# Loading the input by channel instead of transposing it, and shorter arithmetic in the norms, in a hybrid decoder layer

## The chip, the cores and the metric

The kernel runs on one core of one Trainium2 chip. The metric is the device time of one execution in microseconds (us), the median over several executions. Lower is better.

## What is computed

One decoder layer on 256 tokens of 2048 channels, all in float32, batch 1. Three sub-layers follow one another, and each ends in a layer norm over a scaled residual:

```python
h = x
h = _layer_norm(DEEPNORM_ALPHA * h + 0.5 * _swiglu(h, ffn1_w_gate, ffn1_w_up, ffn1_w_down), ln_ffn1_g, ln_ffn1_b)
mix = _mixer(h, ...)      # sparse attention and dilated attention, gated and projected
h = _layer_norm(DEEPNORM_ALPHA * h + mix, ln_mix_g, ln_mix_b)
h = _layer_norm(DEEPNORM_ALPHA * h + 0.5 * _swiglu(h, ffn2_w_gate, ffn2_w_up, ffn2_w_down), ln_ffn2_g, ln_ffn2_b)
```

`_swiglu(x)` is `(silu(x @ w_gate) * (x @ w_up)) @ w_down` with a hidden width of 5632. `_layer_norm` subtracts the mean, multiplies by `rsqrt(var + 1e-5)`, then by a vector g, and adds a vector b. The mixer adds two small position tables (32 x 128) to windows of keys and values before it compresses them.

## The kernel before

**The products.** Every large product multiplies activations that lie with channels on the partitions (`act_hi`, `act_lo`, `hT_hi`, `hT_lo`) with weights that come from HBM. float32 precision is kept by splitting both sides: hi is the value rounded to float32r, lo is the rest. A product is hi x hi, lo x hi and hi x lo, so each pair of a 128x128 block of activations and a 128x512 block of weights takes three matmuls.

**Slots.** Weights come in slots of 2 x 128 rows and 512 columns (512 KB). SyncE (SP) issues one load for each slot into a ring `raw` of 4 (`load_slot`, L469). ScalarE (ACT) rounds a slot into `w_hi` (`round_slot`, L491), VectorE (DVE) writes the rest into `w_lo` (`split_slot`, L505), and TensorE (PE) does 12 matmuls on it (`multiply_slot`, L511, or `first_chunk_slot`, L1625, for the first eight slots). Three waits tie the engines together. The load of slot n waits until the split of slot n-4 is done (`lo_done`, L471). The rounding of slot n waits until PE has used slot n-4 (`slots_used`, L501). The split waits for the rounding, PE for both.

**Order of the first stage.** A feed-forward stage (`ffn`) takes 11 chunks of 512 hidden columns. A chunk is 8 slots of the gate's weights (half 0) and 8 slots of the up weights (half 1), so chunk 0 is slots 0 to 15. After slot 9 has been rounded, ACT takes the tanh of the gate's sums (L841), which waits for PE to have used slot 7, and DVE multiplies by it (L1070); only then come the roundings and splits of slots 10 and 11. Chunk 0 of the first stage is written out by hand ("peel"), the other ten are a loop. Then four chunks of 22 slots each go through the down weights and are added to the residual `resid` (`add_chunk`).

**The input.** x is loaded by token into `resid`, in five pieces of columns (`load_x`, L705) that SP issues between the first slots. PE transposes it, two blocks of channels at a time (`x_task`, L1584: four 128x128 transposes each, eight tasks in all), into PSUM banks. ACT rounds a pair into `act_hi` (L598), DVE writes the rest into `act_lo` (L608). The transposes need the identity `ident`, SP's second load (L717). While no input is there PE multiplies zeros (`keep_warm`, L1610), 6 times before the first transposes and 5 times after them.

**The vectors.** g and b of the first two norms and both position tables are loaded as rows (`load_vectors`, L734, six loads after the load of slot 4). `setup_task` (L1704), right after slot 7 on PE, transposes them into a bank, and DVE copies them into `vecT` (L1059). The same vectors are also loaded broadcast over all partitions into `ln_nat` (`load_ln`, L756), for the residual; SP issues the first pair of these, 1 MB each as written, right after the load of slot 15.

**Norms.** DVE sums the last columns, takes statistics and adds eps to the variance (`sum_last`, `variance`), ACT takes the square root s (`deviation`), and DVE corrects 1/s by one Newton step: a reciprocal and three small operations that wait for one another (`inverse_deviation`, L1159). The last norm (`last_norm`, L1187) multiplies (x - mean) by g over 512 and then over 1536 columns (`scaled`), while ACT does the correction in four small steps (`factor`, L899). Then four `finish` operations of 512 columns multiply by the factor and add b; after each of them SP or ACT, in turns, stores that piece of 256 KB.

**Bank order.** `plan` numbers all uses of the four PSUM banks ahead of time; engines wait for those numbers.

Of the kernel before, what the change touches and what calls it, by code (L numbers as in the profile page):

```python
# [49 lines left out]
X_PARTS = ((0, 256), (256, 512), (512, 1024), (1024, 1536), (1536, D))  # L50
# [76 lines left out]
class Plan:  # L127


    def __init__(self):  # L130
        self.k, self.uses, self.t, self.at, self.by_pos = 0, [0] * BANKS, {}, {}, {}
        self.turn = list(range(BANKS))
# [9 lines left out]
def plan():  # L142
# [10 lines left out]
    def ffn(f):  # L153
        for j in range(GU_SLOTS):
            task(("x", f, j), j % BANKS)
        if f == 0:
            task(("setup",), 2)
# [100 lines left out]
def build(nc, x, w1_gate, w1_up, w1_down, ln1_g, ln1_b, w_in, ck_pos, ck_w1, ck_w2, cv_pos, cv_w1, cv_w2,  # L258
          w_a, w_b, w_o, ln2_g, ln2_b, w2_gate, w2_up, w2_down, ln3_g, ln3_b, rope_c, masks_c, small_c, out):

    (w1_gate, w1_up, w1_down, ln1_g, ln1_b, w_in, ck_pos, ck_w1, ck_w2, cv_pos, cv_w1, cv_w2, w_a, w_b, w_o,
     ln2_g, ln2_b, w2_gate, w2_up, w2_down, ln3_g, ln3_b) = (
        a[0] for a in (w1_gate, w1_up, w1_down, ln1_g, ln1_b, w_in, ck_pos, ck_w1, ck_w2, cv_pos, cv_w1, cv_w2,
# [4 lines left out]
    with ctx:  # L268
# [9 lines left out]
        pos_rows = sb("pos_rows", [CMP_BLOCK, 2, P])  # L278
# [5 lines left out]
        at = 1152 + 4 * (160 + 128 + 256 + 128 + 48 + 16 + 8)  # L284
# [69 lines left out]

        def chunk_buf(order):
            b = CHUNK_BUF[order]
            return chunks_lo[:, b] if b < 8 else chunks_hi[:, b - 8]
# [32 lines left out]
        x_loaded = [sem(f"x_loaded{q}") for q in range(len(X_PARTS))]  # L390
# [12 lines left out]
        three_halves = sem("three_halves")  # L403
# [300 lines left out]
        def _(sp):  # L704
            def load_x(q):  # L705
                cs = slice(*X_PARTS[q])
                sp.dma_start(resid[:, :, cs], x[0].rearrange("(t p) d -> p t d", p=P)[:, :, cs]) \
                    .then_inc(x_loaded[q], 16)
# [25 lines left out]
            def load_vectors():  # L734
                for v, a in enumerate((ln1_g, ln1_b, ln2_g, ln2_b)):
                    sp.dma_start(vec_rows[16 * v:16 * v + 16, :], a.rearrange("(t p) -> t p", p=P)) \
                        .then_inc(consts_loaded, 16)
                sp.dma_start(pos_rows[:, 0, :], ck_pos).then_inc(consts_loaded, 16)
                sp.dma_start(pos_rows[:, 1, :], cv_pos).then_inc(consts_loaded, 16)
# [75 lines left out]
            for tile in range(TILES):  # L815
                for n in range(0, len(OUT_PIECES), 2):
# [5 lines left out]
        def _(act):  # L822
            def gu_chunk(f, i, peel):
                per, c0 = 2 * GU_SLOTS, gu_acc[f]
                for s in range(2 * GU_SLOTS):
                    if peel and f == 0 and s <= X_FIRST:
# [5 lines left out]
                    if peel and f == 0 and X_FIRST < s < GU_SLOTS:  # L832
                        x_pairs(s)
# [26 lines left out]
            def x_pairs(j):  # L860

                round_pair(act, ("x", 0, j), pair_of(act_hi, 2 * j))
# [30 lines left out]
            def deviation(which, tile):  # L893
# [3 lines left out]
                                     bias=ln_s[:, 6, which % 2:which % 2 + 1]).then_inc(std_ready, 1)  # L897

            def factor(tile):  # L899

                at = slice(tile, tile + 1)
                var, r, t, inv = (ln_s[:, k, at] for k in (0, 1, 2, 3))
                act.wait_ge(three_halves, 1)
                act.wait_ge(recip_ready, tile + 1)
                nc.scalar.activation(t, var, ACT.Copy, scale=r).then_inc(factor_step, 1)
                act.wait_ge(factor_step, 4 * tile + 1)
                nc.scalar.activation(t, t, ACT.Copy, scale=r).then_inc(factor_step, 1)
                act.wait_ge(factor_step, 4 * tile + 2)
                nc.scalar.activation(t, t, ACT.Identity, scale=-0.5, bias=ln_s[:, 7, 1:2]).then_inc(factor_step, 1)
                act.wait_ge(factor_step, 4 * tile + 3)  # L910
                nc.scalar.activation(inv, r, ACT.Copy, scale=t).then_inc(factor_step, 1)

            def layer_norm_act(which):

                f, n0 = ("mix", 1)[which], (mix_slot, gu_slot[1])[which]
                for s in range(SPARE):
# [109 lines left out]
            for tile in range(TILES):  # L1026
                deviation(2, tile)
                factor(tile)
                for n in range(1, len(OUT_PIECES), 2):
# [4 lines left out]
        def _(dve):  # L1034
# [8 lines left out]
            def gu_chunk(f, i, peel):  # L1043
                per = 2 * GU_SLOTS
                for s in range(2 * GU_SLOTS):
                    if peel and f == 0 and s <= X_FIRST:
# [5 lines left out]
                    if peel and f == 0 and X_FIRST < s < GU_SLOTS:  # L1052
                        x_pairs(s)
                    if peel and f == 1 and SPLIT <= s < GU_SLOTS:
                        split_piece(1, s + SPLIT)
                    if f == 0 and peel and s == 11:
# [999 lines left out]
```

## Time and profile before

| | |
|---|---|
| median of 3 runs | 2217.81 us (2217.52 to 2217.85) |
| the profiled execution's own time | 2217.98 us |
| its span, from the first instruction to the last | 2216.2 us |
| PE busy | 2201.7 us (99%) |
| DVE, ACT, POOL busy | 1235.7, 959.6, 7.7 us |
| mean granted clock of TensorE | 0.998 of full speed |
| HBM read, mean rate | 418 MB, 190 GB/s over the span |

A time of the profile is counted from the start of the span. What lies outside the span is 2217.98 - 2216.2 = 1.8 us. A busy engine is one that has an instruction in work; matmuls are pipelined, so that the sum of their durations is longer than the time from one start to the next. Two facts of the listing matter below: a float32 matmul of zeros (L1613) leaves two records, and issues of loads stand under SPq and ACTq, the sequencers.

### The profile page before, as it was taken

How to read it: one execution, taken by the hardware profiler on the slowest of the kernel's cores; microseconds unless marked ns; L12 is line 12 of the kernel's file. 1: busy time of each engine (PE TensorE's matmuls, PEld its weight loads, DVE VectorE, ACT ScalarE, POOL GpSimd, SP SyncE). 2: the span in 40 equal slices, each digit the busy share in tenths (PEclk: the TensorE clock that was granted, in tenths of full speed). 3: DMA queues.
4: the chain of work that ended last, by engine and by line, in shares of the span. 5: the costliest groups of instructions: out<-in, count | busy, mean ns of one | idle time of the engine just before them, and what ended most of it. 6: DMA issues, size and time to landing. Idle time of an engine off the chain costs nothing.

```text
span 2216.2 us, 27207 instructions
## 1 busy us (share of the span) xinstructions
PE 2201.7 (99%) x10137; PEld 1823.6 (82%) x10137; DVE 1235.7 (56%) x1230; ACT 959.6 (43%) x1126; POOL 7.7 (0%) x12
## 2 busy tenths in 40 slices
PE   9999999999999999999999999999999999999998
PEld 7888888888888888888888888888888888888886
DVE  5555455544544776776654556567555545545445
ACT  4344434443333644544345444364444444443333
POOL 0000000000000010000000000000000000000000
PEclk9999999999999999999999999999999999999999
DMA  7655665565666666665557566656655566566664
GB/s 270 206 184 188 190 191 185 188 191 190 195 192 193 186 188 206 188 184 161 169 163 208 171 204 206 196 166 195 197 188 180 188 197 188 180 236 193 196 191 142
DMA packets 224860, 422.86 MB, mean 191 GB/s; under 512 B 16400, under 2 KB 25872, under 8 KB 224016
## 3 DMA queue, kind: packets, MB, share of 16 engines
q1 hardware_dynamic: 224208, 420.76, 61.7%
q8 instruction: 52, 0.85, 0.2%
q10 hardware_dynamic: 576, 1.05, 0.1%
q14 instruction: 24, 0.20, 0.0%
HBM read 418.08 MB, written 3.68 MB: 190 GB/s over the span
## 4 chain that ended last, share of the span: by engine, by line
PE 98%; DVE 1%; ACT 0%; DMA 0%; issue 0%; SPq 0%; DVEq 0%; ACTq 0%
PE acc L519 31%; PE acc L520 31%; PE acc L525 31%; PE bank L558 1%; PE bank L1903 1%; PE bank L1743 0%; PE bank L1852 0%; PE bank L1874 0%; PE acc L1640 0%; PE acc L1641 0%; PE bank L1957 0%; PE acc L1647 0%; PE bank L1954 0%; DMA raw<-in_ffn_w_gate_dram 0%; PE bank L1856 0%; DVE w_lo L509 0%
## 5 line engine op out<-in xcount | busy, mean ns | idle before, releaser
L509 DVE TENSOR_TENSOR w_lo<-raw,w_hi 128x1024 fp32r<-128x1024 f32 x768 | 928.3, 1224 | 572.3 <-ACT w_hi L502 564.5
L502 ACT ACTIVATE w_hi<-raw 128x1024 fp32r<-128x1024 f32 x766 | 802.9, 1059 | 820.9 <-PE acc L525 775.0
L519 PE MATMUL acc<-w_hi,act_hi 128*128 128x512 f32 x2192 | 865.9, 395 | 0.0
L520 PE MATMUL acc<-w_hi,act_lo 128*128 128x512 f32 x2192 | 854.3, 390 | 0.0
L525 PE MATMUL acc<-w_lo,act_hi 128*128 128x512 f32 x2192 | 588.2, 389 | 0.1
L525 PEld LDWEIGHTS acc<-w_lo,act_hi 128*128 128x128 f32 x2192 | 411.3, 188 | 87.4 <-DVE w_lo L509 1.0
L519 PEld LDWEIGHTS acc<-w_hi,act_hi 128*128 128x128 f32 x2192 | 411.7, 188 | 86.7 <-issue 3.2
L520 PEld LDWEIGHTS acc<-w_hi,act_lo 128*128 128x128 f32 x2192 | 411.9, 188 | 82.1
L519 PE MATMUL acc<-w_hi,hT_hi 128*128 128x512 f32 x688 | 267.9, 389 | 0.0
L520 PE MATMUL acc<-w_hi,hT_lo 128*128 128x512 f32 x688 | 267.7, 389 | 0.0
L525 PE MATMUL acc<-w_lo,hT_hi 128*128 128x512 f32 x688 | 185.2, 389 | 0.0
L525 PEld LDWEIGHTS acc<-w_lo,hT_hi 128*128 128x128 f32 x688 | 129.2, 188 | 26.8
L520 PEld LDWEIGHTS acc<-w_hi,hT_lo 128*128 128x128 f32 x688 | 129.2, 188 | 26.7
L519 PEld LDWEIGHTS acc<-w_hi,hT_hi 128*128 128x128 f32 x688 | 129.1, 188 | 26.7
L1089 DVE TENSOR_TENSOR hT_lo<-bank,hT_hi 128x512 f32 (+1 forms) x44 | 30.3, 688 | 97.2 <-ACT hT_hi L858 97.2
L1070 DVE SCALAR_TENSOR_TENSOR gate_t<-gate_t,acc 128x1024 f32<-128x1024 f32 x22 | 26.9, 1222 | 88.7 <-ACT gate_t L841 88.7
L858 ACT ACTIVATE hT_hi<-bank 128x512 f32 (+1 forms) x44 | 26.2, 595 | 108.0 <-PE bank L558 108.0
L1081 DVE TENSOR_TENSOR hid<-gate_t,acc 128x1024 f32<-128x1024 f32 x22 | 26.9, 1222 | 65.0 <-PE acc L525 65.0
L841 ACT ACTIVATE gate_t<-acc 128x1024 f32<-128x1024 f32 x22 | 22.6, 1029 | 92.1 <-PE acc L525 90.1
L519 PE MATMUL acc<-w_hi,oT_hi 128*128 128x512 f32 x96 | 38.0, 395 | 0.0
L520 PE MATMUL acc<-w_hi,oT_lo 128*128 128x512 f32 x96 | 37.4, 390 | 0.0
L689 ACT ACTIVATE s<-s,negmax 128x128 f32<-128x128 f32 (+1 forms) x56 | 23.8, 430 | 26.8 <-DVE negmax L1310 26.8
(243 smaller groups left out, 842.2 us busy)
## 6 DMA issues: line engine op xcount, KB each, us to landing
raw<-in_ffn_w_up_dram SPq DMA_DIRECT2D x176, 512.0 KB, 4.5
raw<-in_ffn_w_down_dram SPq DMA_DIRECT2D x176, 512.0 KB, 4.5
raw<-in_w_in_dram SPq DMA_DIRECT2D x176, 512.0 KB, 4.2
raw<-in_ffn_w_gate_dram SPq DMA_DIRECT2D x174, 512.0 KB, 4.5
raw<-in_w_o_dram SPq DMA_DIRECT2D x32, 512.0 KB, 4.8
raw<-in_w_branch_a_dram SPq DMA_DIRECT2D x16, 512.0 KB, 5.1
raw<-in_cmp_k_w_dram SPq DMA_DIRECT2D x8, 512.0 KB, 4.0
raw<-in_cmp_v_w_dram SPq DMA_DIRECT2D x8, 512.0 KB, 4.0
```

Of the source, the lines that this page charges most:

```text
L502: nc.scalar.activation(weights(n0, s if isinstance(i, int) and i == 0 else s + per)[0], raw[:, r, :], ACT.Copy).then_inc(hi_done, 1)
L509: nc.vector.tensor_tensor(lo, raw[:, r, :], hi.bitcast(F32), ALU.subtract).then_inc(lo_done, 1)
L519: nc.tensor.matmul(o, a_hi[:, kt0 + k, at], hi, start=first and k == 0, stop=False)
L520: nc.tensor.matmul(o, a_lo[:, kt0 + k, at], hi, start=False, stop=False)
L525: mm = nc.tensor.matmul(o, a_hi[:, kt0 + k, at], lo, start=False, stop=last and k == SLOT_KT - 1)
L558: mm = nc.tensor.transpose(bank[:, b, k * TOKENS + tile * P:k * TOKENS + (tile + 1) * P], src[:, tile, col + k * P:col + (k + 1) * P], ident)
L689: nc.scalar.activation(v, v, ACT.Exp, bias=negmax[:, u, e:e + 1], scale=SCALE, accum_out=sums[:, u, e:e + 1]).then_inc(probs_ready, 1)
L841: nc.scalar.activation(gate_t[:, :, :], acc_pair(0), ACT.Tanh, scale=0.5).then_inc(gate_tanh, 1)
L858: nc.scalar.activation(dst, bank[:, half, :].rearrange("p (k n) -> p k n", k=2), ACT.Copy).then_inc(hi_moved, 1)
L1070: nc.vector.scalar_tensor_tensor(gate_t[:, :, :], gate_t[:, :, :], 1.0, acc_pair(0), ALU.add, ALU.mult).then_inc(acc_emptied[0], 1)
L1081: nc.vector.tensor_tensor(hid[:, :, :], gate_t[:, :, :], acc_pair(1), ALU.mult).then_inc(acc_emptied[1], 1)
L1089: nc.vector.tensor_tensor(hT_lo[:, k0, :], bank[:, half, :].rearrange("p (k n) -> p k n", k=2), hT_hi[:, k0, :].bitcast(F32), ALU.subtract ...
```

## The change

- The host hands over x a second time, rearranged so that a partition holds a channel (`x_by_channel`), and one array `vectors` that has g, b and the position tables in the layout of `vecT`. The original x is still an input.
- SP loads x by channel into `x_raw`, which lies in the space of `hT_hi`, in eight loads of 256 KB, each ahead of the load of the slot that uses it. ACT rounds from there into `act_hi` (512 columns each) and DVE writes the rest into `act_lo`; no transposes. On ACT and DVE the pair of slot s comes ahead of slot s for all eight (before, from slot 3 on, behind it).
- PE's eight `x_task`s and the `setup_task` are gone, and with them the copy L1059. PE multiplies zeros 8 times. In the first eight slots PE does the hi x hi of both tiles before the lo x hi, with a wait for `act_lo` between.
- The identity and the vectors are loaded after the load of slot 15, ahead of the broadcast vectors. PE waits for the identity right after slot 7, where `setup_task` was.
- x by token is loaded whole (2 MB) between the gate/up loop and the down slots of the first stage; the first `add_chunk` waits for it.
- Norms: ACT takes the square root of a quarter of the variance, s/2; the factor is 1 / (s/2 + (v/4) / (s/2)). That is a reciprocal, one operation and a reciprocal on DVE; in the last norm the middle one is on ACT, in place of four there, and DVE takes the second reciprocal.
- The last norm scales and finishes in turns: scale 0 to 512, scale 512 to 1024, finish both, scale and finish 1024 to 1536, scale 1536 to 2048, finish 256 columns and 256 columns. Five stores in place of four.

```diff
-OUT_PIECES = ((0, 512), (512, 1024), (1024, 1536), (1536, D))
+OUT_PIECES = ((0, 512), (512, 1024), (1024, 1536), (1536, 1792), (1792, D))
-WARM_START = (6, 5)
-X_FIRST = 2
+WARM_START = 8
...
@@ @block.sync @@
-            def load_x(q):
-                cs = slice(*X_PARTS[q])
-                sp.dma_start(resid[:, :, cs], x[0].rearrange("(t p) d -> p t d", p=P)[:, :, cs]) \
-                    .then_inc(x_loaded[q], 16)
+            def load_x(j):
+                sp.dma_start(pair_of(x_raw, 2 * j), xT_c[:, 2 * j * TOKENS:(2 * j + 2) * TOKENS]).then_inc(x_loaded[j], 16)
...
-            load_x(0)
-            sp.dma_start(ident, small_c[:, n_small:]).then_inc(small_loaded, 16)
...
+                        if peel:
+                            load_x(s)
                         if peel and s < IN_HALVES:
                             first_weights(s)
                         else:
                             load_slot(sp, src, gu_slot[f], i, 2 * GU_SLOTS, h * GU_SLOTS + s)
-                        if peel:
-                            for q in ((1,), (2,), (), (3, 4))[s] if s < 4 else ():
-                                load_x(q)
-                            if s == 4:
-                                load_vectors()
...
+            def load_constants():
+                sp.dma_start(ident, small_c[:, n_small:]).then_inc(small_loaded, 16)
+                sp.dma_start(vecT[:, :], vec_c).then_inc(consts_loaded, 16)
 
             def ffn(f):
                 gu_chunk(f, 0)
                 if f == 0:
+                    load_constants()
                     load_ln(0)
                 with sp.Fori(1, GU_CHUNKS) as i:
                     gu_chunk(f, i)
-                if f == 1:
+                if f == 0:
+                    sp.dma_start(resid[:, :, :], x[0].rearrange("(t p) d -> p t d", p=P)).then_inc(resid_loaded, 16)
+                else:
                     sp.wait_ge(resid_ready, 2)
                     load_ln(2)
...
@@ @block.scalar @@
             def x_pairs(j):
 
-                round_pair(act, ("x", 0, j), pair_of(act_hi, 2 * j))
+                act.wait_ge(x_loaded[j], 16)
+                nc.scalar.activation(pair_of(act_hi, 2 * j), pair_of(x_raw, 2 * j), ACT.Copy).then_inc(hi_moved, 1)
...
             def factor(tile):
...
+                quarter_var, r, t, half_std = (ln_s[:, k, tile:tile + 1] for k in (0, 1, 2, 5))
                 act.wait_ge(recip_ready, tile + 1)
-                nc.scalar.activation(t, var, ACT.Copy, scale=r).then_inc(factor_step, 1)
-                act.wait_ge(factor_step, 4 * tile + 1)
-                nc.scalar.activation(t, t, ACT.Copy, scale=r).then_inc(factor_step, 1)
-                act.wait_ge(factor_step, 4 * tile + 2)
-                nc.scalar.activation(t, t, ACT.Identity, scale=-0.5, bias=ln_s[:, 7, 1:2]).then_inc(factor_step, 1)
-                act.wait_ge(factor_step, 4 * tile + 3)
-                nc.scalar.activation(inv, r, ACT.Copy, scale=t).then_inc(factor_step, 1)
+                nc.scalar.activation(t, quarter_var, ACT.Identity, scale=r, bias=half_std).then_inc(factor_step, 1)
...
@@ @block.vector @@
             def x_pairs(j):
 
-                split_pair(dve, ("x", 0, j), pair_of(act_lo, 2 * j), pair_of(act_hi, 2 * j))
+                dve.wait_ge(hi_moved, moved[("x", 0, j)] + 1)
+                nc.vector.tensor_tensor(pair_of(act_lo, 2 * j), pair_of(x_raw, 2 * j), pair_of(act_hi, 2 * j).bitcast(F32),
+                                        ALU.subtract).then_inc(x_split, 1)
...
-                link(nc.vector.reciprocal(r, ln_s[:, 5, at]))
-                link(nc.vector.scalar_tensor_tensor(t, r, var, r, ALU.mult, ALU.mult))
-                link(nc.vector.tensor_scalar(t, t, -0.5, 1.5, ALU.mult, ALU.add))
-                link(nc.vector.tensor_tensor(inv, r, t, ALU.mult))
+                link(nc.vector.reciprocal(r, half_std))
+                link(nc.vector.scalar_tensor_tensor(t, quarter_var, r, half_std, ALU.mult, ALU.add))
+                link(nc.vector.reciprocal(inv, t))
...
-                scaled(tile, D // 4, D)
-                dve.wait_ge(factor_step, 4 * tile + 4)
-                for lo, hi in OUT_PIECES:
-                    finish(tile, lo, hi)
+                scaled(tile, *OUT_PIECES[1])
+                dve.wait_ge(factor_step, tile + 1)
+                link(nc.vector.reciprocal(ln_s[:, 3, tile:tile + 1], ln_s[:, 2, tile:tile + 1]))
+                finish(tile, *OUT_PIECES[0])
+                finish(tile, *OUT_PIECES[1])
+                scaled(tile, *OUT_PIECES[2])
+                finish(tile, *OUT_PIECES[2])
+                scaled(tile, OUT_PIECES[3][0], D)
+                finish(tile, *OUT_PIECES[3])
+                finish(tile, *OUT_PIECES[4])
...
@@ @block.tensor @@
                         if f == 0:
                             first_chunk(n0, c0)
-                            setup_task()
+                            pe.wait_ge(small_loaded, 16)
```

## Rows read from the trace of the kernel before

**Rows 1.** Part 1 of the page, the engines' busy time, and part 4, the chain
```profile
PE 2201.7 (99%) x10137; PEld 1823.6 (82%) x10137; DVE 1235.7 (56%) x1230; ACT 959.6 (43%) x1126; POOL 7.7 (0%) x12
...
PE 98%; DVE 1%; ACT 0%; DMA 0%; issue 0%; SPq 0%; DVEq 0%; ACTq 0%
```

**Rows 2.** Waits of PEld, whole span: us in total, times, longest
```profile
PEld acc L519 <- DVE act_lo L1100: 2.4, 8, 0.5
```

**Rows 3.** Timeline, start: start us, us, engine, line, operation [idle before <-releaser]
```profile
5.29 0.69 DVE L608 SCALAR_TENSOR_TENSOR act_lo<-bank,act_hi 128x512 fp32r<-128x512 f32 x1 [4.25 <-ACT act_hi L598]
5.45 0.63 ACT L848 ACTIVATE w_hi<-raw 128x512 fp32r<-128x512 f32 x1 [0.20 <-DMA raw<-in_ffn_w_gate_dram]
...
7.14 0.63 ACT L850 ACTIVATE w_hi<-raw 128x512 fp32r<-128x512 f32 x1 [1.06 <-DMA raw<-in_ffn_w_gate_dram]
...
7.88 1.23 DVE L509 TENSOR_TENSOR w_lo<-raw,w_hi 128x1024 fp32r<-128x1024 f32 x1 [1.91 <-ACT w_hi L850]
...
9.21 1.17 PE L1647 MATMUL acc<-w_lo,act_hi 128*128 128x512 f32 x4
```

**Rows 4.** Timeline, last four matmuls of slots 5, 6 and 7
```profile
26.20 1.08 PE L1647 MATMUL acc<-w_lo,act_hi 128*128 128x512 f32 x4
...
29.41 1.08 PE L1647 MATMUL acc<-w_lo,act_hi 128*128 128x512 f32 x4
...
32.13 1.07 PE L1647 MATMUL acc<-w_lo,act_hi 128*128 128x512 f32 x4
```

**Rows 5.** Timeline, from slot 7's end to the loads behind slot 15
```profile
33.24 1.03 ACT L841 ACTIVATE gate_t<-acc 128x1024 f32<-128x1024 f32 x1 [2.07 <-PE acc L1647]
...
33.57 0.50 PE L519 MATMUL acc<-w_hi,act_hi 128*128 128x512 f32 x1
...
34.30 1.22 DVE L1070 SCALAR_TENSOR_TENSOR gate_t<-gate_t,acc 128x1024 f32<-128x1024 f32 x1 [1.69 <-ACT gate_t L841]
...
35.44 2.35 DVE L509 TENSOR_TENSOR w_lo<-raw,w_hi 128x1024 fp32r<-128x1024 f32 x2
...
38.23 0.47 SPq L759 DMA_DIRECT2D ln_nat<-in_ln_ffn_g_dram  x1
```

**Rows 6.** DMA issues, first 60 us: engine, count, KB each, median us to landing
```profile
raw<-in_ffn_w_up_dram SPq DMA_DIRECT2D x8, 512.0 KB, 4.5
ln_nat<-in_ln_ffn_g_dram SPq DMA_DIRECT2D x1, 1024.0 KB, 8.3
...
small<-in_small_dram SPq DMA_DIRECT2D x1, 64.0 KB, 2.6
vec_rows<-in_ln_ffn_g_dram SPq DMA_DIRECT2D x1, 8.0 KB, 6.9
```

**Rows 7.** PE groups by form, windows 1 to 4 and 4 to 6: count | busy, mean ns
```profile
L1613 PE MATMUL bank<-hid 128*128 128x128 f32 x12 | 2.9, 435 | 1.1 <-DVE ln_s L1257 1.1
...
L1613 PE MATMUL bank<-hid 128*128 128x128 f32 x10 | 1.3, 275 | 0.0
```

**Rows 8.** Stretches at the end: PE, PEld, DVE, ACT, POOL busy, granted clock, DMA share, GB/s
```profile
2206.00:2208.00 2.00, 0.00 (x0) 0.00 (x0) 1.90 (x5) 0.29 (x1) 0.00 (x0) 1.00 0.00 0
2208.00:2210.00 2.00, 0.00 (x0) 0.00 (x0) 1.97 (x3) 1.18 (x4) 0.00 (x0) 0.76 0.00 0
```

**Rows 9.** Timeline, last small operation of the first norm's correction
```profile
737.57 0.16 DVE L1168 TENSOR_TENSOR ln_s<-ln_s 128x1 f32<-128x1 f32 x1
```

**Rows 10.** Timeline, the last norm's second tile behind PE's last matmuls
```profile
2205.01 0.61 PE L525 MATMUL acc<-act_lo,hT_hi 128*128 128x512 f32 x2
...
2207.48 0.74 DVE L1179 SCALAR_TENSOR_TENSOR resid<-resid,mv,ln_nat 128x512 f32<-128x512 f32 x1
...
2208.34 1.80 DVE L1179 SCALAR_TENSOR_TENSOR resid<-resid,mv,ln_nat 128x1536 f32<-128x1536 f32 x1
...
2210.17 2.74 DVE L1184 SCALAR_TENSOR_TENSOR resid<-resid,ln_s,ln_nat 128x512 f32<-128x512 f32 x4
```

**Rows 11.** DMA issues, 2205 to 2217 us, the columns of Rows 6
```profile
out_dram<-resid ACTq DMA_DIRECT2D x2, 256.0 KB, 2.8
```

More of the change, by code:

```diff
@@ L153, in ffn @@
     def ffn(f):
-        for j in range(GU_SLOTS):
+        for j in range(GU_SLOTS if f else 0):
             task(("x", f, j), j % BANKS)
-        if f == 0:
-            task(("setup",), 2)
         for i in range(GU_CHUNKS):
@@ L353, in build @@
         dilw = sb("dilw", [P, 6, 3, 8])
+        x_raw = chunks_lo[:, 0:4].rearrange("p a t (k n) -> p (a t k) n", n=TOKENS)
         def chunk_buf(order):
@@ L389, in build @@
         hi_moved = sem("hi_moved")
-        x_loaded = [sem(f"x_loaded{q}") for q in range(len(X_PARTS))]
+        x_loaded = [sem(f"x_loaded{j}") for j in range(GU_SLOTS)]
+        x_split = sem("x_split")
+        resid_loaded = sem("resid_loaded")
         small_loaded = sem("small_loaded")
@@ L815, in _ @@
             for tile in range(TILES):
-                for n in range(0, len(OUT_PIECES), 2):
+                for n in (0, 2, 4):
                     store_piece(sp, tile, n)
@@ L825, in gu_chunk @@
                 for s in range(2 * GU_SLOTS):
-                    if peel and f == 0 and s <= X_FIRST:
+                    if peel and f == 0 and s < GU_SLOTS:
                         x_pairs(s)
@@ L1028, in _ @@
                 factor(tile)
-                for n in range(1, len(OUT_PIECES), 2):
+                for n in (1, 3):
                     store_piece(act, tile, n)
@@ L1045, in gu_chunk @@
                 for s in range(2 * GU_SLOTS):
-                    if peel and f == 0 and s <= X_FIRST:
+                    if peel and f == 0 and s < GU_SLOTS:
                         x_pairs(s)
@@ L1051, in gu_chunk @@
                         split_slot(dve, gu_slot[f], i, per, s)
-                    if peel and f == 0 and X_FIRST < s < GU_SLOTS:
-                        x_pairs(s)
                     if peel and f == 1 and SPLIT <= s < GU_SLOTS:
                         split_piece(1, s + SPLIT)
-                    if f == 0 and peel and s == 11:
-                        t = T[("setup",)]
-                        wait_filled(dve, t)
-                        nc.vector.tensor_copy(vecT[:, :], bank[:, t.bank, 0:128]).then_inc(bank_emptied[t.bank], 1)
                     if peel and f == 1 and s >= 10:
@@ L1155, in variance @@
                 dve.wait_ge(var_ready, 2 * which + tile + 1)
-                nc.vector.tensor_scalar(ln_s[:, 0, tile:tile + 1], mv[:, tile, 1:2], EPS * UNIT[which] ** 2, None, ALU.add) \
+                nc.vector.tensor_scalar(ln_s[:, 0, tile:tile + 1], mv[:, tile, 1:2], EPS * UNIT[which] ** 2, 0.25,
+                                        ALU.add, ALU.mult) \
                     .then_inc(var_biased, 1)
@@ L1221, in down @@
                     if end == DOWN_SLOTS - 1 and c >= 0:
+                        if c == 0 and f == 0:
+                            dve.wait_ge(resid_loaded, 16)
                         if c == 0 and f == 1:
@@ L1255, in _ @@
             nc.vector.memset(hid[:, 0, 0:P], 0.0).then_inc(zeros_ready, 1)
+            for b in range(2):
+                nc.vector.memset(ln_s[:, 0, b:b + 1], 0.0).then_inc(bank_emptied[b], 1)
             for k in range(2):
-                nc.vector.memset(ln_s[:, 6, k:k + 1], EPS * UNIT[k] ** 2).then_inc(zeros_ready, 1)
-            nc.vector.memset(ln_s[:, 7, 1:2], 1.5).then_inc(three_halves, 1)
+                nc.vector.memset(ln_s[:, 6, k:k + 1], 0.25 * EPS * UNIT[k] ** 2).then_inc(zeros_ready, 1)
             gu_chunk(0, 0, True)
@@ L1612, in keep_warm @@
                 for _ in range(n):
-                    nc.tensor.matmul(bank[:, 3, 0:P], hid[:, 0, 0:P], hid[:, 0, 0:P], start=True, stop=True)
+                    mm = nc.tensor.matmul(bank[:, 3, 0:P], hid[:, 0, 0:P], hid[:, 0, 0:P], start=True, stop=True)
+                mm.then_inc(bank_filled, 1)
             def first_chunk(n0, c0):
                 pe.wait_ge(zeros_ready, 1)
-                keep_warm(WARM_START[0])
-                x_task(0, 0)
-                keep_warm(WARM_START[1])
+                keep_warm(WARM_START)
                 for s in range(GU_SLOTS):
-                    wait_moved(pe, T[("x", 0, s)])
                     first_chunk_slot(s, c0 % 2)
@@ L2018, in link @@
                 pool.wait_ge(pool_step, steps[0])
+            pool.wait_ge(consts_loaded, 16)
             for v in range(2):
@@ L2045 @@
     nc = bacc.Bacc("TRN2", target_bir_lowering=False, num_devices=1, dynamic_dma_scratch_size=1024)
-    named = [(name, np.ascontiguousarray(inputs[name])) for name in _INS]
+    x = np.ascontiguousarray(inputs["x"])
+    vectors = [by_partition(np.asarray(inputs[name])) for name in ("ln_ffn1_g", "ln_ffn1_b", "ln_mix_g", "ln_mix_b")]
+    vectors += [np.asarray(inputs[name])[0].T for name in ("cmp_k_pos", "cmp_v_pos")]
+    named = [("x", x), ("x_by_channel", by_partition(x[0])), ("vectors", np.ascontiguousarray(np.concatenate(vectors, 1)))]
+    named += [(name, np.ascontiguousarray(inputs[name])) for name in _INS]
     named += list(zip(("rope", "masks", "small"), mixer_constants()))
```

69 lines of the change are left out of this document (20 added, 49 removed).

## Prediction

> **What bounds the kernel.** I read the page first. PE is busy for 99% of the span and holds 98% of the chain that ended last [rows 1]. So a change counts only where it takes work off PE, lets PE start earlier, makes PE wait, or changes what follows PE's last matmul. Next the list of waits: nothing is waited for long in the middle. The one row that bears on the norms is 2.4 us of idle on PE's weight loads, in eight short pieces, and most of that lies under running matmuls [rows 2]. That leaves the two ends of the timeline, and I read those closely.
>
> At the start everything waits for data: ACT rounds the first half slot at 5.45 us and the second at 7.14, each as soon as its DMA had landed, and PE follows [rows 3]. From slot 3 on PE runs without a gap. The last four matmuls of slots 5 and 6 are 3.21 us apart, those of slots 6 and 7 2.72 us, because slot 7 alone has no transposes between its matmuls [rows 4]. So a slot is worth 2.72 us and a transpose task 0.49 us. The last matmul of slot 7 ends at 33.20 us, and the first of slot 8 starts at 33.57 us [rows 4, 5]. I call the end of slot 7 T8: everything below hangs on it.
>
> **Part 1, the start without transposes.** SP issues x's first piece and then the first half slot directly; before, the identity stood between them. One issue is about 0.5 us (the row of the loads behind slot 15 shows 0.47 [rows 5]). The second half of slot 0 had landed at 7.14 [rows 3], so I take 6.6. Rounding 0.63 and splitting 1.23 [rows 3] end near 8.5, and slot 0's last four matmuls run from 8.6 to 9.5. Before, they started at 9.21 and ended at 10.1. Are slots 1 to 7 then bound by PE? DVE has 0.69 for the pair and 1.23 for the slot [rows 3], 1.9 us in all, and ACT about 1.7: both under 2.72. The DMAs must bring 768 KB a slot, as on average before, now in 2.72 us instead of 3.21; a rival below prices the case that they can't. I take PE as the bound: T8 = 9.5 + 7 x 2.72 = 28.5. The setup task's 0.37 us goes as well. Without anything new, slot 8 would start at 28.5 instead of 33.57: **-5.1 us**. The bounds are -6 (data half a microsecond earlier still) and -3.5 (a slot or two late from DMA).
>
> **Part 2, the new wait.** PE waits for the identity right after slot 7. SP issues that load behind the load of slot 15, which waits for the split of slot 11. Follow it: the tanh of the gate's sums starts when PE has used slot 7 (33.24, 1.03 us), DVE's product follows (34.30, 1.22), and only then the splits of slots 10 and 11 (35.44, 2.35 together), to 37.79 [rows 5]. SP then issues slot 15, and the next thing on its queue starts at 38.23 [rows 5]. In the changed kernel that next thing is the identity. So it is issued at T8 + 5.03 us, and it cannot be issued earlier, since its chain starts at T8 itself. PE's queue meanwhile holds slots 8 to 15, all behind the wait, though the first of them are ready; ACT waits behind PE once its four buffers are full. Nothing covers this: PE is the bound, so an idle microsecond is lost.
>
> How long until it lands is not in the trace, so I bound it. Issued when almost nothing was in flight, the identity took 2.6 us [rows 6]: T8 + 7.6. A small load among many took 6.9 us [rows 6]: T8 + 11.9. Here two up slots are in flight ahead of it, and such a slot takes 4.5 us by the median [rows 6]; the last of them is issued 0.4 us before it. The nearest row is that one, less what the issues are apart and a little more, since no large load shares with it as early as there: 3.6 us, T8 + 8.6. PE stalls for **8.6 us**, bounds 7.6 and 11.9.
>
> A rule that bears on this: the Trainium skill, DMA: Bandwidth & Descriptors, section on queues, rings and completion order, says that each DMA engine consumes descriptors in ring order and that a completion count is written only after that engine's earlier writes. By it the identity cannot land before slot 15, issued ahead of it, which points to the middle value and not to 2.6 us. The row of the broadcast vector, 8.3 us for 1 MB right behind a slot [rows 6], does not contradict it and does not prove it.
>
> **Part 3, the clock.** At the end of the trace PE's last matmul ends at 2205.6 [rows 10]; the granted clock is 1.00 until 2208 and 0.76 on average from 2208 to 2210 [rows 8], so it fell to the lower level about 3.4 us after the last matmul. A stall of 8.6 us is longer, so slot 8 should begin at the lower of the two levels, 1.2 GHz. The price comes from the start: 12 records of zero matmuls took 2.9 us there, and 10 later ones 1.3 us [rows 7], 0.24 against 0.13 us each, half the speed for about 3 us. Half of that is lost: **+1.5 us**. Bounds: 0 (the clock does not fall or is back at once) and 2.5.
>
> The windows around the start show a clock of 1.00 although the matmuls ran at half pace; the Trainium skill, TensorE: Matmul & The Clock Gate, section on the clock gate, says that such trace events have been seen to be unreliable. By that the durations are to be believed there, as I do; by the recorded clock alone the term would be 0 and the sum 1.5 us less.
>
> **Part 4, loads moved.** The 2 MB of x by token are issued ahead of the down slots and used 22 slots later, 22 x 2.72 = 60 us. Weight loads queue behind it for at most some 11 us (2 MB at the span's mean rate of 190 GB/s), but the slots run up to eight ahead, four raw and four rounded, about 20 us. The nearest case is the pair of broadcast vectors, also 2 MB, behind slot 15: no wait of PE for a slot appears there. Cost 0; if the cover were gone, up to 11 us. The vectors' load is needed 700 us later. The copy L1059 and the memsets are under PE's work.
>
> **Part 5, the first two norms.** One small linked operation of 0.16 us plus 0.04 to the next [rows 9] leaves each tile's correction, four in all, 0.8 us on DVE. PE's idle in these places is mostly under matmuls [rows 2]. I take **-0.2 us**, bounds -0.8 and 0.
>
> **Part 6, the last norm.** Before, from 2208.34: 1.80 for 1536 columns, then four finishes of 0.685, to 2212.91 [rows 10]. After: 0.74 for 512 columns [rows 10], to 2209.1; the second reciprocal with its link 0.2 [rows 9]; two finishes 1.37; then twice 0.78 for scaling, 0.69 for a finish, and two finishes of half width. Those have no row; between half and whole they are 0.35 to 0.69, I take 0.4. That gives 2213.7, 0.8 later. ACT's three steps less save nothing, since they ended under the long scaling. The last store is 128 KB in place of 256 KB, which landed after 2.8 us [rows 11]; a 64 KB load took 2.6 [rows 6]. I take 0.3 back: **+0.5 us**, bounds 0 and +1.
>
> **Sum.** -5.1 + 8.6 + 1.5 - 0.2 + 0.5 = +5.3 us. The profiled execution took 2217.98 us (span 2216.2 and 1.8 around it), 0.17 above the median of the runs. So 2217.8 + 5.3 = 2223.1 us.
>
> **The rivals.**
> - Forecast: stall of about 8.6 us and half clock behind it. 2223.1, own range 2221.5 to 2225. Chance 0.55.
> - The identity shares the DMA engines with the two broadcast vectors issued right behind it, as the small vectors did (6.9 us [rows 6]): stall 11.9, +3.3 us, 2226.4. For it: large loads behind one did stretch others here. Against: it is issued a microsecond ahead of them. Chance 0.12.
> - The start is bound by DMA. The trace shows only that 768 KB were brought in 3.21 us [rows 4]. Were that the limit, T8 = 9.5 + 7 x 3.21 = 32.0, 3.5 us later; half of it gives 2224.9. Against: x was brought in by the fourth slot, so the loads ran ahead of 3.21 us for most of the start. Chance 0.10.
> - The short stall: the identity lands 2.6 us after its issue and the clock holds: -1.0 - 1.5, 2220.6. Chance 0.16.
> - Faster: the wait costs nothing, and the transposes' time is kept. This needs the identity landed before T8, that is issued before about 26 us. It would be so if SP reached that load early, with slot 15's load not held by the split of slot 11. Then -5.1 - 0.2 + 0.5 = -4.8, 2213.0. Against: the chain of part 2, in which every link is a wait in the code. Chance 0.07.
>
> About 0.2%, 4.4 us, is what a measurement of this kernel can tell from no change; that is 2213.4 and 2222.2. Faster has most of the last rival, 0.05. Within are its rest, the short stall and the lower part of the forecast, 0.02 + 0.16 + 0.12 = 0.30. Slower is the remainder, 0.65. The range 2219.5 to 2227 leaves out the faster rival and the far end of the long stall.
>
> **What the profile would show.** Slot 7's last matmul near 28.5 us and none of line 558 before it; then a PE idle of 8 to 9 us released by the DMA into `small`, issued 5.0 us after slot 7's end; a granted clock near 0.5 at its end and in the first 3 us of slot 8, with matmuls 0.43 us apart instead of 0.23; slot 8 near 37 us instead of 33.57. From there on everything is later by the same amount up to the last norm. There the last finish should come about 8.1 us after PE's end instead of 7.3. I am wrong if PE goes on at T8 within a microsecond, if T8 is above 30, or if the down slots wait for the 2 MB load.

## The result, and the profile after

The changed kernel takes 2225.58 us (median of 7 runs, 2224.59 to 2226.49), the kernel before 2217.87 (7 runs, 2217.52 to 2218.12) in the same comparison. The ratio is 1.0034, 95% interval 1.0025 to 1.0044: slower by 7.7 us, 0.3%, and clear of the spread of both kernels' runs. The forecast was 2223.1, with a range of 2219.5 to 2227. The profiled execution took 2225.58 us, its span is 2223.6.

Part 1 and part 4 of the page of the changed kernel, where [rows 1] stood for the kernel before:

```profile
PE 2200.0 (99%) x10096; PEld 1821.7 (82%) x10096; DVE 1236.4 (56%) x1234; ACT 957.7 (43%) x1120; POOL 7.7 (0%) x12
...
PE 98%; DVE 1%; DMA 1%; ACT 0%; SPq 0%; issue 0%; DVEq 0%; ACTq 0%
```

PE is busy for less time than before, 2200.0 us against 2201.7, and yet the span is 7.4 us longer. One per cent of the chain is now DMA. The list of waits of PE over the whole span (us in total, times, longest) says which:

```profile
PE acc L517 <- DMA small<-in_small_dram: 9.7, 1, 9.7
PE bank L1921 <- DVE w_lo L507: 1.1, 2, 0.8
PE bank L1591 <- DVE ln_s L1246: 1.1, 1, 1.1
```

A single wait of 9.7 us for the identity. The second and third lines were there before, with the same sizes. The timeline of the changed kernel from slot 7's end, all engines, beside [rows 5]:

```profile
27.79 1.07 PE L1620 MATMUL acc<-w_lo,act_hi 128*128 128x512 f32 x4
28.89 1.02 ACT L830 ACTIVATE gate_t<-acc 128x1024 f32<-128x1024 f32 x1 [3.99 <-PE acc L1620]
...
29.95 1.22 DVE L1047 SCALAR_TENSOR_TENSOR gate_t<-gate_t,acc 128x1024 f32<-128x1024 f32 x1 [3.78 <-ACT gate_t L830]
31.09 2.35 DVE L507 TENSOR_TENSOR w_lo<-raw,w_hi 128x1024 fp32r<-128x1024 f32 x2
33.88 0.47 SPq L726 DMA_DIRECT2D small<-in_small_dram  x1
...
38.52 0.79 PE L517 MATMUL acc<-w_hi,act_hi 128*128 128x512 f32 x1 [9.67 <-DMA small<-in_small_dram]
39.12 0.63 PE L518 MATMUL acc<-w_hi,act_lo 128*128 128x512 f32 x1
...
43.77 0.39 PE L517 MATMUL acc<-w_hi,act_hi 128*128 128x512 f32 x1
44.00 0.39 PE L518 MATMUL acc<-w_hi,act_lo 128*128 128x512 f32 x1
```

Read it as a chain. Slot 7's last matmul ends at 28.86. The tanh, the product, the splits of slots 10 and 11 follow as they did before, and the identity is issued at 33.88, 5.02 us after slot 7's end. Behind slot 8's first matmul the step from one matmul to the next is about 0.43 us, and 0.23 us again in slot 9, which starts at 43.77. The stretches of the changed kernel show why (columns as in [rows 8]):

```profile
30.00:32.00 2.00, 0.00 (x0) 0.00 (x0) 2.00 (x2) 1.81 (x2) 0.00 (x0) 1.00 0.06 24
32.00:34.00 2.00, 0.00 (x0) 0.00 (x0) 1.44 (x2) 0.00 (x0) 0.00 (x0) 0.87 0.37 31
...
40.00:42.00 2.00, 2.00 (x6) 1.61 (x5) 0.00 (x0) 0.00 (x0) 0.00 (x0) 0.50 0.99 418
42.00:44.00 2.00, 2.00 (x6) 1.52 (x6) 0.00 (x0) 0.00 (x0) 0.00 (x0) 0.57 0.30 127
44.00:46.00 2.00, 2.00 (x10) 1.68 (x9) 0.87 (x1) 1.06 (x1) 0.00 (x0) 1.00 0.01 4
```

The granted clock fell in the stall and came back only after some 5 us of work. The issues of DMAs in the first 60 us, beside [rows 6] (KB each, us to landing):

```profile
small<-in_small_dram SPq DMA_DIRECT2D x1, 64.0 KB, 4.6
```

The load of slot 15, issued 0.41 us ahead of the identity, first in the timeline and then in the list of DMA issues around it:

```profile
33.47 0.37 SPq L472 DMA_DIRECT2D raw<-in_ffn_w_up_dram  x1
```

```profile
raw<-in_ffn_w_up_dram SPq DMA_DIRECT2D x1, 512.0 KB, 4.8
```

So slot 15 landed at 38.27 us and the identity at 38.48, and PE went on at 38.52.

The other end of the trace, DVE behind PE's last matmul, beside [rows 10]:

```profile
2214.86 0.74 DVE L1158 SCALAR_TENSOR_TENSOR resid<-resid,mv,ln_nat 128x512 f32<-128x512 f32 x1
...
2216.68 1.42 DVE L1163 SCALAR_TENSOR_TENSOR resid<-resid,ln_s,ln_nat 128x512 f32<-128x512 f32 x2
...
2219.46 0.74 DVE L1158 SCALAR_TENSOR_TENSOR resid<-resid,mv,ln_nat 128x512 f32<-128x512 f32 x1
2220.24 0.88 DVE L1163 SCALAR_TENSOR_TENSOR resid<-resid,ln_s,ln_nat 128x256 f32<-128x256 f32 x2
```

From PE's last matmul (2213.00) to the last finish (2221.12) are 8.12 us, against 7.29 before. But the span ends 2.48 us behind the last finish, against 3.29. The two cancel.

### The profile page after: what moved, and what is told of

It reads as the page before. It is cut to its first block, busy times and chain, and to the rows that moved or that the text cites. A ratio compares the mean times of both kernels' runs of the same rounds, so it can differ in the third digit from the quotient of the medians.

```text
span 2223.6 us, 27137 instructions
## 1 busy us (share of the span) xinstructions
PE 2200.0 (99%) x10096; PEld 1821.7 (82%) x10096; DVE 1236.4 (56%) x1234; ACT 957.7 (43%) x1120; POOL 7.7 (0%) x12
## 3 DMA queue, kind: packets, MB, share of 16 engines
HBM read 420.18 MB, written 3.68 MB: 191 GB/s over the span
## 4 chain that ended last, share of the span: by engine, by line
PE 98%; DVE 1%; DMA 1%; ACT 0%; SPq 0%; issue 0%; DVEq 0%; ACTq 0%
PE acc L517 31%; PE acc L518 31%; PE acc L523 30%; PE bank L556 1%; PE bank L1867 1%; PE bank L1707 0%; PE bank L1816 0%; PE bank L1838 0%; DMA raw<-in_ffn_w_gate_dram 0%; PE bank L1921 0%; DVE w_lo L507 0%; PE bank L1918 0%; PE acc L1613 0%; PE acc L1620 0%; PE acc L1616 0%; DMA small<-in_small_dram 0%
```

## The experiments

All kernels below except before_with_wait are edits of the changed kernel. The kernel before took 2217.82 us beside the first four, 2217.90 beside the next four and 2217.95 beside the last two. Ratios are to that.

**wait_later** moves one line.

```diff
@@ behind slot 7 @@
-                            pe.wait_ge(small_loaded, 16)
...
             def ffn(f):
                 gu_chunk(f, 0, True)
+                if f == 0:
+                    pe.wait_ge(small_loaded, 16)
                 with pe.Fori(1, GU_CHUNKS) as i:
```

> The changed kernel with PE's wait for the identity moved from behind slot 7 to ahead of the loop, behind slot 15, where the identity is first needed. Theory (the wait is the whole loss, a stall of 9.67 us and 2.4 us of half clock, and all else of the change gains 4.7 us at the start and nothing at the end): no stall, clock at the full level through slot 8, slot 8's first matmul near 28.7 us, about 2225.6 - 12.1 = 2213.5 us, faster than the kernel before by 4.4. Rival (the start without transposes costs something later, or the norms and the last norm lose time that the stall hides): slot 8 at 28.7 all the same but above 2215.

Measured: 2213.14 us (2212.39 to 2213.47), ratio 0.9979 (0.9970 to 0.9988). That is 12.4 us less than the changed kernel and 4.7 less than the kernel before. The timeline of this kernel, PE at slot 7's end:

```profile
27.06 1.07 PE L1620 MATMUL acc<-w_lo,act_hi 128*128 128x512 f32 x4
27.96 0.39 PE L517 MATMUL acc<-w_hi,act_hi 128*128 128x512 f32 x1
28.19 0.39 PE L518 MATMUL acc<-w_hi,act_lo 128*128 128x512 f32 x1
```

Slot 8 follows slot 7 without a gap and at full pace. The identity's load was issued as late as before, and nobody waited for it. The rival falls.

**ident_earlier** leaves the wait and moves the load ahead, behind the load of slot 7.

```diff
                             load_slot(sp, src, gu_slot[f], i, 2 * GU_SLOTS, h * GU_SLOTS + s)
+                        if peel and s == GU_SLOTS - 1:
+                            sp.dma_start(ident, small_c[:, n_small:]).then_inc(small_loaded, 16)
...
             def load_constants():
-                sp.dma_start(ident, small_c[:, n_small:]).then_inc(small_loaded, 16)
```

> The changed kernel with the wait left where it is and the identity's load issued behind the load of slot 7 instead of slot 15. Theory (it is the place on SP's queue that makes the stall): the identity is issued near 16 us and lands well before slot 7's end, no stall, within 0.3 us of the run with the wait moved, about 2213.5. Rival (the wait itself or the identity's own landing is slow): a stall of over 2 us remains, above 2215.5.

Measured: 2213.18 us (2212.88 to 2213.60), ratio 0.9979 (0.9970 to 0.9988). No wait for the identity is left, though its load took 5.2 us to land here, longer than in the changed kernel. So neither the wait nor the landing makes a stall by itself; it is the place on SP's queue, behind a load that waits for PE's own progress.

**before_with_wait** puts only the suspected part into the kernel before.

```diff
@@ sync, behind the load of slot 15 @@
                 if f == 0:
+                    sp.dma_start(ident, small_c[:, n_small:]).then_inc(small_loaded, 16)
                     load_ln(0)
@@ tensor @@
                             first_chunk(n0, c0)
+                            pe.wait_ge(small_loaded, 32)
                             setup_task()
```

> The kernel before, with its transposes, with the identity loaded a second time behind slot 15 and PE waiting for that second load behind slot 7, nothing else changed. Theory (the stall and the clock behind it are the whole cost and do not depend on the rest of the change): + 9.7 for the stall, + 2.4 for the half clock, about 2230. Rival (the landing is slow only because of the new loads around it): stall near 7.6 us and less for the clock, below 2228.

Measured: 2230.63 us (2229.55 to 2230.78), ratio 1.0057 (1.0043 to 1.0071): + 12.8 us, where the changed kernel with the wait and without it differ by 12.4. PE's wait, and the first and the eighth matmul of slot 8 in this kernel:

```profile
42.82 0.37 PE L1711 MATMUL bank<-small,vec_rows 64*128 64x64 f32 x1 [9.99 <-DMA small<-in_small_dram]
...
43.46 0.80 PE L519 MATMUL acc<-w_hi,act_hi 128*128 128x512 f32 x1
...
46.62 0.63 PE L520 MATMUL acc<-w_hi,act_lo 128*128 128x512 f32 x1
```

A stall of 10.0 us and half pace after it, with none of the change's new loads around. The wait costs nearly the same in both kernels, and everything else of the change is worth -4.7 us without the wait (wait_later against the kernel before) and -5.1 with it (the changed kernel against this one).

**zeros_in_stall** separates the clock from the stall: PE works on zeros while it would wait.

```diff
                             first_chunk(n0, c0)
+                            for _ in range(36):
+                                nc.tensor.matmul(bank[:, 3, 0:P], hid[:, 0, 0:P], hid[:, 0, 0:P], start=True, stop=True)
                             pe.wait_ge(small_loaded, 16)
```

> The changed kernel with 36 multiplications of zeros on PE between slot 7 and the wait, some 9.2 us at full clock, so that PE works while it would stand still. Theory (behind the stall the matmuls are slow because the clock fell while PE was idle): the stall's time stays, granted clock 1.00 in slot 8, matmuls 0.23 us apart there instead of 0.43, 2.4 us faster than the changed kernel: 2223.2. Rival (slot 8 is slow for another reason, the two broadcast loads that land in the same microseconds): slot 8 takes 5.2 us again, 2225.6.

Measured: 2225.16 us (2222.97 to 2226.78), ratio 1.0032 (1.0019 to 1.0044). Taken alone the time would speak for the rival. The timeline tells otherwise: the zeros ended after 8.2 us and the identity landed late, 5.1 us after its issue, so that an idle of 2.2 us was left. The timeline of this kernel and two of its stretches:

```profile
28.72 8.20 PE L1666 MATMUL bank<-hid 128*128 128x128 f32 x72
39.08 0.50 PE L517 MATMUL acc<-w_hi,act_hi 128*128 128x512 f32 x1 [2.16 <-DMA small<-in_small_dram]
39.41 0.49 PE L518 MATMUL acc<-w_hi,act_lo 128*128 128x512 f32 x1
39.70 0.63 PE L517 MATMUL acc<-w_hi,act_hi 128*128 128x512 f32 x1
```

```profile
38.00:40.00 2.00, 0.93 (x3) 0.78 (x4) 0.00 (x0) 0.00 (x0) 0.00 (x0) 0.89 0.92 335
40.00:42.00 2.00, 2.00 (x6) 1.52 (x6) 0.00 (x0) 0.00 (x0) 0.00 (x0) 0.50 1.02 430
```

Slot 8's first two matmuls are still quick, 0.3 us from one to the next; from the third on the step is 0.43. The mean of 0.89 between 38 and 40 puts the fall of the clock at about 39.6 us, 0.5 us into the slot and 2.6 us behind the last zeros. The experiment had left a gap, and so did not separate the two.

**zeros_longer** closes the gap.

```diff
-                            for _ in range(36):
+                            for _ in range(46):
```

> As zeros_in_stall, with 46 multiplications of zeros, 10.4 us, so that no idle is left before slot 8 (there 2.2 us were left, and the granted clock fell all the same). Theory (the clock falls with PE's idle, however the idle comes): granted clock 1.00 through slots 8 and 9, slot 8 in 2.7 us, slot 8's first matmul near 28.7 + 10.4 = 39.1 us, and 2.4 - 0.7 = 1.7 us faster than the changed kernel: 2223.9. Rival (the two broadcast loads slow it): slot 8 above 4 us again.

Measured: 2223.59 us (2223.14 to 2224.28), ratio 1.0026 (1.0016 to 1.0036), against the 2223.9 expected. Its timeline, and a stretch in which the two broadcast loads are landing at 416 GB/s:

```profile
38.76 0.48 PE L517 MATMUL acc<-w_hi,act_hi 128*128 128x512 f32 x1
...
41.57 0.39 PE L517 MATMUL acc<-w_hi,act_hi 128*128 128x512 f32 x1
```

```profile
38.00:40.00 2.00, 2.00 (x15) 1.79 (x15) 0.00 (x0) 0.00 (x0) 0.00 (x0) 1.00 1.00 416
```

Slot 8 takes 2.8 us and the clock is 1.00, with the same loads in flight. The slow slot 8 is the clock's doing and not the DMAs', and the clock stays up when PE has no gap.

**old_last_norm** starts from wait_later and undoes the turns and the fifth piece.

```diff
-                scaled(tile, *OUT_PIECES[1])
+                scaled(tile, D // 4, D)
                 dve.wait_ge(factor_step, tile + 1)
                 link(nc.vector.reciprocal(ln_s[:, 3, tile:tile + 1], ln_s[:, 2, tile:tile + 1]))
-                finish(tile, *OUT_PIECES[0])
...
+                for lo, hi in OUT_PIECES:
+                    finish(tile, lo, hi)
```

> The kernel with the wait moved, with the last norm in the order of before (scale 512, scale 1536, then the finishes) and four pieces again; the new factor stays. Theory (in turns costs 0.8 us on DVE and gives 0.8 back at the last store): PE's last matmul to the last finish about 7.5 us (7.25 before, and the second reciprocal), the last store 3.3 us behind it, the median within 0.4 us of the kernel with the wait moved, 2213.1 to 2213.5. Rival (in turns is a gain because stores start earlier): over 0.6 us slower, above 2213.7.

Measured: 2213.20 us (2213.11 to 2214.30), ratio 0.9979 (0.9970 to 0.9988): no difference to 2213.14. By its trace the last finish ends 7.49 us behind PE's last matmul and the span 3.20 us behind that, 10.69 in all; in turns it was 8.13 and 2.56, also 10.69.

**five_in_order** has the order of before and the five pieces (the edit of old_last_norm with `OUT_PIECES` of the change).

> The kernel with the wait moved, with the order of before in the last norm but the five pieces of the change. Theory (what the change wins at the end comes from the small last store alone, and the turns only cost): the last finish 0.4 to 0.5 us earlier than in turns, the last store as short, 0.5 us faster than the kernel with the wait moved: 2212.6. Rival (stores issued closer together queue behind one another and take the gain back): within 0.2 us of it, 2213.1.

Measured: 2213.77 us (2213.02 to 2214.45), ratio 0.9981 (0.9972 to 0.9990). The theory fails, and in the rival's direction or beyond. Stores of this kernel, then of wait_later (KB each, us to landing):

```profile
out_dram<-resid ACTq DMA_DIRECT2D x1, 128.0 KB, 3.1
out_dram<-resid SPq DMA_DIRECT2D x1, 128.0 KB, 3.0
```

```profile
out_dram<-resid ACTq DMA_DIRECT2D x1, 128.0 KB, 2.0
out_dram<-resid SPq DMA_DIRECT2D x1, 128.0 KB, 2.1
```

The last finish came 0.5 us earlier (7.62 us behind PE instead of 8.13), but the two 128 KB stores land 1.0 us later each. Medians 0.6 us apart would be a thin proof, since the start alone varies by more (last section). The traces carry it: from PE's last matmul to the span's end this kernel takes 11.05 us, against 10.69 in wait_later and old_last_norm. In both orders the two small stores are issued 0.4 us apart. What differs is the 256 KB store ahead of them: it is issued 1.2 us ahead of the first in turns, 0.4 us here. The turns do buy something: they keep that distance, and that pays for the longer DVE work.

**three_small_ops_more** starts from wait_later and adds small work to the first two norms.

```diff
                 link(nc.vector.scalar_tensor_tensor(t, quarter_var, r, half_std, ALU.mult, ALU.add))
+                link(nc.vector.tensor_scalar(t, t, 1.0, None, ALU.mult))
+                link(nc.vector.tensor_scalar(t, t, 1.0, None, ALU.mult))
+                link(nc.vector.tensor_scalar(t, t, 1.0, None, ALU.mult))
                 link(nc.vector.reciprocal(inv, t))
```

> The kernel with the wait moved, with three more small linked operations on DVE in each tile's correction of the first two norms (twelve in all; the change took four away). They multiply by 1. Theory (these norms hide DVE's small work, so the shorter correction gained nothing): below 0.4 us slower, 2213.1 to 2213.5. Rival (DVE is on the path there, 0.2 us for each operation): each norm shifts by 0.6 us a tile, 1.2 to 2.4 us slower, 2214.3 to 2215.5, which would mean that the change did gain 0.4 to 0.8 us there.

Measured: 2214.07 us (2213.62 to 2214.79), ratio 0.9983 (0.9974 to 0.9992), 0.9 us more than wait_later. It lies between the two expectations. By the traces the time from slot 8 to PE's last matmul grows from 2171.85 to 2172.70 us, 0.85 us for twelve operations, 0.07 each, where an operation and its link last 0.2. In the other kernels of this section that have neither a stall of PE nor longer norms this stretch is 2171.83 to 2171.92, so the 0.85 is no scatter. DVE is on the path in a part of these places.

**zeros_for_transposes** gives the first slots back the work that the transposes were.

```diff
                 for k in range(SLOT_KT):
+                    if k and s < GU_SLOTS - 1:
+                        for _ in range(2):
+                            nc.tensor.matmul(bank[:, 3, 0:P], hid[:, 0, 0:P], hid[:, 0, 0:P], start=True, stop=True)
```

> The kernel with the wait moved, with two multiplications of zeros in each of slots 0 to 6, where a transpose task stood before: 0.46 us for each slot, about what a task cost (0.49). Theory (the start gained because slots 1 to 7 are bound by PE, so the transposes' time came off the path one for one): 5 to 7 of the 7 count, 2.3 to 3.2 us slower, 2215.5 to 2216.4. Rival (the start gained because the data is there earlier, and PE waits for loads between the slots): the zeros fall into waits and cost below 1.2 us, under 2214.4.

Measured: 2215.73 us (2215.44 to 2217.40), ratio 0.9992 (0.9983 to 1.0001). 2.6 us more than wait_later is 5.6 of the seven pairs at 0.46 us. In the trace slots 1 to 6 take 3.18 us each with the zeros, where slots without them take 2.72, and PE waits for no data behind slot 0. So over half of the start's gain of 4.7 us is the transposes' own time on PE. The missing 1.4 pairs would fit the first slots, where without the zeros PE waits for data; no run takes the rest of the gain apart.

**x_twice_and_wait** tests the cover of the moved 2 MB load.

```diff
                     sp.dma_start(resid[:, :, :], x[0].rearrange("(t p) d -> p t d", p=P)).then_inc(resid_loaded, 16)
+                    sp.wait_ge(resid_loaded, 16)
+                    sp.dma_start(resid[:, :, :], x[0].rearrange("(t p) d -> p t d", p=P)).then_inc(resid_loaded, 16)
```

> The kernel with the wait moved, with x by token loaded twice (4 MB), SP waiting for the first load before it issues the second; the down slots' loads stand behind both. Theory (slots run up to eight ahead of PE, some 20 us, and cover the moved load): first down slot late by about 8 us for the wait and by the second 2 MB, no wait of PE, within 0.3 us of the kernel with the wait moved, 2212.8 to 2213.4. Rival (the cover is thinner, and the 2 MB load alone used it up): PE waits for a rounded slot behind the loop, several us slower, above 2215.

Measured: 2219.49 us (2217.94 to 2220.87), ratio 1.0007 (0.9998 to 1.0016), 6.3 us more than wait_later. PE's wait, a stretch with the granted clock, SP's issues of x and ACT's first rounding of a down slot in this kernel:

```profile
PE acc L517 <- ACT w_hi L500: 3.4, 1, 3.4
```

```profile
499.00:501.00 2.00, 1.91 (x5) 1.55 (x6) 1.94 (x2) 1.57 (x2) 0.00 (x0) 0.50 1.04 402
```

```profile
479.13 0.38 SPq L737 DMA_DIRECT2D resid<-in_x_dram  x1
488.62 0.38 SPq L739 DMA_DIRECT2D resid<-in_x_dram  x1
```

```profile
497.89 1.06 ACT L500 ACTIVATE w_hi<-raw 128x1024 fp32r<-128x1024 f32 x1 [11.98 <-DMA raw<-in_ffn_w_down_dram]
```

And the same in the changed kernel, where the load is issued once:

```profile
490.71 0.38 SPq L737 DMA_DIRECT2D resid<-in_x_dram  x1
```

```profile
502.40 1.06 ACT L500 ACTIVATE w_hi<-raw 128x1024 fp32r<-128x1024 f32 x1 [4.90 <-DMA raw<-in_ffn_w_down_dram]
```

With one load the first down slot is rounded 11.7 us after x's issue, and PE does not wait. With two and the wait between it is 18.8 us, and PE waits 3.4. So PE would begin to wait at some 15.4 us (18.8 less the wait): the moved load is hidden, with 3.7 us to spare and not more. The rival was right that the cover is thinner than claimed; its second half, that one load used it up, is not.

## Why the prediction was right, step by step

- **Part 1, the start.** Forecast -5.1 us, from slot 8 at 28.5. Measured: slot 7 ends at 28.86, -4.7. The data did come earlier than I wrote (slot 0's last matmuls started at 7.59 and not 8.6), but 1.0 us was lost again between the starts of slots 1 and 2 (3.68 us instead of 2.72), where ACT's roundings waited for their loads. The two cancel, and that is luck. zeros_for_transposes shows that the transposes' time came off for 5.6 of seven slots. The -4.7 is one trace's; by the starts of slot 8 in the last section the gain lies between -3.9 and -5.6.
- **Part 2, the stall.** The chain was as predicted to the hundredth: issue 5.02 us after slot 7's end, 5.03 forecast. The landing was the mis-sized term: 4.6 us after the issue, where I took 3.6. The stall was 9.7 us and not 8.6, within the bounds of 7.6 and 11.9. In all eleven traces with a load of the identity behind a slot's it took 4.6 to 5.2 us, near the median of the up slots (4.5 [rows 6]), from which I had talked myself down: I took off what the issues are apart, and then half a microsecond more for the absence of large loads. The Trainium skill's rule (DMA: Bandwidth & Descriptors, queues, rings and completion order), that a completion count is written only after that engine's earlier writes, kept me off the short value. The traces agree with it: in each of the eleven the identity landed 0.1 to 0.5 us behind the slot issued 0.4 us ahead of it, 38.48 behind 38.27 in the changed kernel. Even the 2.6 us of the kernel before fit: that load landed 0.2 us behind the 256 KB of x ahead of it. By that order the term would have been 4.5 - 0.4 + 0.2 = 4.3 us. No run took the slot ahead away, so that the identity waits for it is the likeliest reading and not shown alone.
- **Part 3, the clock.** The mechanism is shown by zeros_longer. The size was off: slot 8 took 5.25 us (38.52 to 43.77) against 2.86 before (33.57 [rows 5] to slot 9's start at 36.43, the row below), +2.4 us where I took 1.5. I had priced 3 us at half pace from the zeros at the start [rows 7]; it was over 5 us. The 3.4 us from the last matmul to the clock's fall, read at the end of the kernel before, was no constant either: by the means of the stretches it was 4.6 us in this stall, 2.6 in zeros_in_stall and 2.4 in x_twice_and_wait. The conclusion drawn from it held, since the stall was longer than any of these.

```profile
36.43 0.39 PE L519 MATMUL acc<-w_hi,act_hi 128*128 128x512 f32 x1
```

- **Part 4, moved loads.** Cost 0, as forecast: PE waits for no down slot in the changed kernel. But the cover was given as about 20 us, and x_twice_and_wait puts it at 15.4.
- **Part 5, the first norms.** Forecast -0.2. From slot 9's start to PE's last matmul it was 2169.19 us before and 2169.13 in wait_later: -0.06. The twelve added operations cost 0.07 each, which would make four worth 0.28. The two differ, and whether the gain is 0.06 or 0.28 us, or between, stays open.
- **Part 6, the last norm.** Forecast +0.5, of which DVE +0.8 and the store -0.3. DVE came out at +0.83. The end of the span came 0.8 us closer to the last finish, where I took 0.3; without the spacing of the stores the small piece alone gains nothing (five_in_order). Sum 0.
- **The sum.** -4.7 + 9.7 + 2.4 + 0 = +7.4 us of span, and 0.2 us more outside it: +7.6, against +5.3. The likeliest case held in its mechanism; its two largest new costs were each about 1 us too small, and the gain at the start 0.4 too large. The result, 2225.58, lies 0.6 us above that case's own range (2221.5 to 2225) and inside the whole range (to 2227); the 0.5 us of part 6 that did not come kept it from going further.
- **The faster rival** named the right price for the kernel without the wait, 2213.0, which wait_later and ident_earlier then gave (2213.14 and 2213.18). Both beat the kernel before and the changed kernel.

## What to carry to other kernels

When a load is moved down a queue, look at what the queue's earlier entries wait for: if one of them waits for the progress of the engine that will wait for the load, the stall has a minimum that no spare time covers. Here it was 5.0 us until the issue and 4.6 until the landing, 9.7 us for a 64 KB load. Put a wait at the first use of what is waited for, not at the place where the old code stood. And price an idle of PE with the clock behind it. That price does not follow the length of the idle: it was 2.4 us behind a stall of 9.7, some 2.9 behind a wait of 3.4 (x_twice_and_wait) and 1.7 behind a gap of 2.2 (zeros_in_stall).

## What the runs showed that I had not expected

- **A short idle was enough for the clock.** In zeros_in_stall PE stood still for 2.16 us, behind 8.2 us of zero matmuls of 128 columns, and the granted clock fell to half 0.5 us into slot 8, when PE was at work again; the slot took 4.45 us. The zeros alone were not the cause, since in zeros_longer 10.4 us of them without a gap left the clock at 1.00. In x_twice_and_wait PE waited 3.4 us behind real work, and the kernel is 6.3 us slower by the medians; from slot 8 to PE's last matmul its trace takes 6.4 us more than that of wait_later. The clock read 0.50 behind the wait, and the first down slot took 5.26 us in place of 2.72.
- **The start varies more.** Slot 8 began at 27.96, 28.33, 28.79, 29.47 and 29.72 us in five traces in which nothing ahead of slot 7 differs. The spread of the changed kernel's runs is 1.9 us, that of the kernel before 0.6. Without the transposes PE follows the first loads more closely, and PE's waits for rounded slots there differ from trace to trace (0.3 us in wait_later; 0.7 and 0.3 in ident_earlier).
- **Small stores pay for closeness.** The two last stores of 128 KB landed in 2.0 and 2.1 us where the 256 KB store ahead of them had been issued 1.2 us earlier, and in 3.1 and 3.0 us where it had been issued 0.4 us earlier.
